# A macaron encoder layer: the mixing stage between its two feed-forward blocks written out in a new order

## What is computed

```python
x = x + 0.5 * swiglu(rmsnorm(x, ffn1_norm), ...)
h = rmsnorm(x, mix_norm)
p = h @ w_in                       # 1024 -> 3072: q | k | v | hyena x0 | x1 | v, 512 each
# differential attention, 4 heads, each with two 64-wide softmaxes over a T5 bias
attn = softmax(logits[0]) - lam * softmax(logits[1])
out = rmsnorm(attn @ v, subln_g) * (1.0 - lambda_init)      # norm over the 128 values of a head
# hyena: short convolution of width 3 on x0, x1, v; then
v = v * x1
v = irfft(rfft(v) * rfft(kernel)) + v * filt_bias           # kernel from a small MLP
y = rmsnorm_by_group(v * x0, out_g)                         # groups of 64 channels
x = x + concat([out, y]) @ w_out                            # 1024 -> 1024
x = x + 0.5 * swiglu(rmsnorm(x, ffn2_norm), ...)
x = rmsnorm(x, final_norm)
```

## Time and profile before

| | us |
|---|---|
| median of 3 runs (1060.88 to 1065.59) | 1061.97 |
| the profiled execution, its own time | 1061.0 |
| its span, first to last instruction | 1059.2 |
| TensorE busy | 1034.5 (98%) |
| VectorE busy | 569.8 (54%) |
| ScalarE busy | 335.2 (32%) |
| GpSimd busy | 60.7 (6%) |

### The profile page before, as it was taken

The page is one execution under the profiler, slowest core; times in us unless marked ns, Lnnn a source line. Parts: engine busy times, 40 slices in busy tenths (PEclk is TensorE's granted clock), DMA queues, the critical chain, the costliest instruction groups (busy, mean ns, idle before and its releaser), DMA issues. The chain is left out here.

```text
span 1059.2 us, 12002 instructions
## 1 busy us (share of the span) xinstructions
PE 1034.5 (98%) x4551; PEld 821.8 (78%) x4551; DVE 569.8 (54%) x722; ACT 335.2 (32%) x477; POOL 60.7 (6%) x57
## 2 busy tenths in 40 slices
PE   9999999999999999999999969999999999999996
PEld 8887888888777867777775558878888888888885
DVE  5545444454544458695876695764544444433332
ACT  6222222222222333444444203532222222222222
POOL 0000000000000010000000160300000000000000
PEclk9999999999999999999999989999999999999999
DMA  7743332333233361322211000323333333333322
GB/s 221 165 118 90 100 99 86 98 95 101 83 94 105 90 199 40 97 78 80 80 60 40 1 20 21 99 87 98 94 99 99 99 99 90 96 97 91 94 70 79
DMA packets 184460, 96.69 MB, mean 91 GB/s; under 512 B 14811, under 2 KB 181859, under 8 KB 184424
## 3 DMA queue, kind: packets, MB, share of 16 engines
q1 hardware_dynamic: 183160, 92.70, 30.2%
q0 software_dynamic: 352, 1.85, 0.6%
q10 hardware_dynamic: 912, 1.64, 0.5%
HBM read 94.07 MB, written 2.11 MB: 91 GB/s over the span
## 5 line engine op out<-in xcount | busy, mean ns | idle before, releaser
L1137 PE MATMUL bank<-x_hi,w_hi 128*128 128x512 f32 x880 | 347.0, 394 | 0.8 <-DVE x_lo L748 0.4
L1139 PE MATMUL bank<-x_hi,w_lo 128*128 128x512 f32 x880 | 342.6, 389 | 0.0
L1138 PE MATMUL bank<-x_lo,w_hi 128*128 128x512 f32 x880 | 342.6, 389 | 0.0
L713 DVE TENSOR_TENSOR w_lo<-raw,w_hi 128x1024 fp32r<-128x1024 f32 x168 | 203.6, 1212 | 220.9 <-ACT w_hi L447 216.5
L447 ACT CAST w_hi<-raw 128x1024 fp32r<-128x1024 f32 x168 | 172.3, 1026 | 167.4 <-PE bank L1139 131.8
L1137 PEld LDWEIGHTS bank<-x_hi,w_hi 128*128 128x128 f32 x880 | 165.2, 188 | 43.2 <-issue 7.0
L1139 PEld LDWEIGHTS bank<-x_hi,w_lo 128*128 128x128 f32 x880 | 165.2, 188 | 34.7
L1138 PEld LDWEIGHTS bank<-x_lo,w_hi 128*128 128x128 f32 x880 | 165.3, 188 | 34.6 <-issue 1.2
L1137 PE MATMUL bank<-h_hi,w_hi 128*128 128x512 f32 x352 | 137.3, 390 | 0.0
L1139 PE MATMUL bank<-h_hi,w_lo 128*128 128x512 f32 x352 | 137.0, 389 | 0.0
L1138 PE MATMUL bank<-h_lo,w_hi 128*128 128x512 f32 x352 | 136.9, 389 | 0.0
(11 more groups left out here) (207 smaller groups left out, 783.3 us busy)
## 6 DMA issues: line engine op xcount, KB each, us to landing
raw<-in_ffn_w_gate SPq DMA_DIRECT2D x44, 512.0 KB, 3.8
raw<-in_ffn_w_up SPq DMA_DIRECT2D x44, 512.0 KB, 3.7
raw<-in_ffn_w_down SPq DMA_DIRECT2D x32, 512.0 KB, 3.5
raw<-in_w_in SPq DMA_DIRECT2D x24, 512.0 KB, 3.7
raw<-in_ffn_w_down SPq DMA_DIRECT2D x16, 384.0 KB, 3.0
raw<-in_w_out SPq DMA_DIRECT2D x8, 512.0 KB, 3.4
x_nat<-in_x SPq DMA_DIRECT2D x4, 512.0 KB, 7.1
out<-o_nat SPq DMA_DIRECT2D x8, 256.0 KB, 2.9
```

The costliest lines, as they stand in the source:

```text
L713: nc.vector.tensor_tensor(w_lo[:, half, 0:kb, :], raw[:, slot, 0:kb, :], w_hi[:, half, 0:kb, :].bitcast(F32), ALU.subtract).then_inc(w_spl ...
L1137: nc.tensor.matmul(dst, w_hi[:, half, k, :], hi, start=first and k == 0, stop=False)
L1138: nc.tensor.matmul(dst, w_hi[:, half, k, :], lo, start=False, stop=False)
L1139: ins = nc.tensor.matmul(dst, w_lo[:, half, k, :], hi, start=False, stop=last and k == kb - 1)
```

## The change

- The tiles of the projection go in the order of a list `SEQ` of (kind, group) pairs: first x1 and v of the hyena for all four groups, then v, q, k of head 0, x0 of two groups, and so on head by head.
- The filters, the kernel spectra and the turning of the values (`turn_values`) stand between the first eight tiles. The forward transforms, the spectral products and the four inverse transforms stand between the heads of the attention. Products and both sums are all VectorE's; GpSimd's part is gone. The products are cut into small functions (`cross_products` and those behind it) that stand between `logits` and `combine` calls.
- The inverse transform goes by channel group: `inverse(g)` needs both frequency halves of the spectrum (`spec_set` at 2). `attend(2)` uses PSUM bank 4 behind `inverse(0)`, so it waits for `long_read`, which the first `long_out` sets.
- `logits` does the scaling, the bias and the row minimum in one instruction (`tensor_tensor_reduce`). `combine` has one pass over the row fewer, since the common factor of the first softmax is left to the norm.
- `attend` multiplies with `attn_t` as the stationary operand, in 128 columns, so a head's output has its queries on partitions. The sum of squares of the norm then comes out of ScalarE's accumulator (`attended`), the scale is a broadcast along the row (`att_scale`), and `turn_att` turns the result back. The column sums and spreads of the attention are gone; those of the hyena stay.
- The spectra need room, so SyncE writes `resid` (2 MB) to DRAM early in the stage and reads it back behind the last inverse transform; both transfers stand in the queue of the weight loads.
- The output tiles begin with the hyena half, and `OUT_TILES` and `OUT_BANKS` change: two pairs of residual blocks, the third and the fourth, are now handled behind one another at the last tile.

```diff
-OUT_TILES = [(0, 0), (0, 1), (0, 2), (1, 0), (1, 1), (1, 2), (0, 3), (1, 3)]
-OUT_DONE = [OUT_TILES.index((1, pair)) for pair in range(4)]
+OUT_TILES = [(1, 0), (1, 1), (0, 0), (1, 2), (0, 1), (1, 3), (0, 2), (0, 3)]
+OUT_DONE = [OUT_TILES.index((0, pair)) for pair in range(4)]
+SEQ = [(4, 0), (5, 0), (4, 1), (5, 1), (4, 2), (5, 2), (4, 3), (5, 3), (2, 0),
+       (0, 0), (1, 0), (3, 0), (3, 3), (2, 1),
...
@@ SyncE
+            for n, (m, g) in enumerate(SEQ):
+                load(w[:, :, m * D_ATT + g * P:m * D_ATT + (g + 1) * P], KD, N_MIX + n)
+                if n == 3:
+                    sp.wait_ge(resid_set, KD)
+                    sp.dma_start(resid_dram, resid[:]).then_inc(resid_saved, 16)
...
@@ VectorE
-                    nc.vector.scalar_tensor_tensor(logit[:, c, :], bank[2 + c][:], -(DK ** -0.5), near,
-                                                   ALU.mult, ALU.subtract).then_inc(logit_set, 1)
...
-                    nc.vector.tensor_reduce(soft[:, c:c + 1], logit[:, c, :], AX.X, ALU.min).then_inc(max_set, 1)
+                    nc.vector.tensor_tensor_reduce(logit[:, c, :], bank[2 + c][:], near, -(DK ** -0.5), LEAST,
+                                                   ALU.add, ALU.min, stat[:, c:c + 1]).then_inc(logit_set, 1)
...
-                link(nc.vector.tensor_scalar(prob[:, 1, :], prob[:, 1, :], soft[:, 6:7], None, ALU.mult))
+                link(nc.vector.scalar_tensor_tensor(stat[:, 3:4], s0, lam[:, 5:6], stat[:, 2:3], ALU.mult, ALU.mult))
...
+            project(20)
+            split(8, N_MIX + 22)
+            combine(2, 0)
+            taps(20)
+            logits(2, 1)
+            own_products(1)
+            combine(2, 1)
+            project(21)
+            split(8, N_MIX + 23)
+            imaginary(1)
+            logits(2, 2)
+            real(1)
+            combine(2, 2)
+            real_parities(1)
+            logits(2, 3)
+
+            project(22)
+            split(8, N_OUT)
+            imaginary_parities(1)
+            combine(2, 3)
+            split_qk(3, 0)
+            project(23)
+            split(8, N_OUT + 1)
+            split_qk(3, 1)
+            long_out(0)
...
@@ TensorE
+            def attend(h):
                 pe.wait_ge(attn_set, NT * (h + 1))
+                if h < 2:
+                    pe.wait_ge(spec_read, h + 1)
+                else:
+                    pe.wait_ge(long_read, (1, 3)[h - 2])
...
-                    ins = nc.tensor.matmul(bank[6][:], v_nat[:, kt, :], attn_t[:, kt, :], start=kt == 0, stop=kt == NT - 1)
+                    for qb in range(NT):
+                        ins = nc.tensor.matmul(bank[6][:, qb * P:(qb + 1) * P], attn_t[:, kt, qb * P:(qb + 1) * P], v_nat[:, kt, :],
+                                               start=(kt, qb) == (0, 0), stop=(kt, qb) == (NT - 1, NT - 1))
...
+            def inverse(g):
+
+                pe.wait_ge(spec_set, 2)
...
+            project(20)
+            scores(2, 1)
+            project(21)
+            scores(2, 2)
+            project(22)
+            scores(2, 3)
+
+            inverse(0)
+            project(23)
+            attend(2)
+            turn_v(3)
+            pe.wait_ge(qk_split, 8)
+            scores(3, 0)
+            inverse(1)
```

More of the change, by code:

```diff
@@ new lines, in _ @@
+            project(8)
+            split(8, N_MIX + 10)
+            project(9)
+            split(8, N_MIX + 11)
+            project(10)
+            split(8, N_MIX + 12)
+            split_qk(0, 0)
+            split_qk(0, 1)
+            cosines(0)
+            sines(0)
+            logits(0, 0)
+            project(11)
+            split(8, N_MIX + 13)
+            combine(0, 0)
+            taps(11)
+            logits(0, 1)
+            cross_products(0)
+            combine(0, 1)
+            project(12)
@@ new lines, in _ @@
+            split(8, N_MIX + 14)
+            taps(12)
+            logits(0, 2)
+            own_products(0)
+            project(13)
+            split(8, N_MIX + 15)
+            combine(0, 2)
+            imaginary(0)
+            logits(0, 3)
+            project(14)
+            split(8, N_MIX + 16)
+            combine(0, 3)
+            project(15)
+            split(8, N_MIX + 17)
+            split_qk(1, 0)
+            split_qk(1, 1)
+            real(0)
+            real_parities(0)
@@ new lines, in _ @@
+            combine(3, 3)
+            long_out(3)
+            hy_inverse(0)
+            att_scale(0)
+            for g in range(3):
+                hy_scale(g)
+            hy_inverse(1)
+            hy_low(0)
+            hy_low(1)
+            hy_scale(3)
+            hy_low(2)
+            hy_low(3)
+            att_scale(1)
+            att_low(0)
+            att_low(1)
+            split(8, N_OUT + 2)
+            att_low(2)
+            att_low(3)
+            for n in range(2, KD):
@@ new lines, in _ @@
+            project(7)
+            project(8)
+            for g in range(NG):
+                turn_values(g)
+            project(9)
+            project(10)
+            turn_v(0)
+            forward(0)
+            pe.wait_ge(qk_split, 2)
+            scores(0, 0)
+            project(11)
+            scores(0, 1)
+            project(12)
+            scores(0, 2)
+            project(13)
+            scores(0, 3)
+            project(14)
+            project(15)
+            attend(0)
+            turn_v(1)
@@ new lines, in _ @@
+            scores(2, 3)
[5 more added lines that the diff above has]
+            scores(3, 0)
+            inverse(1)
+            scores(3, 1)
+            inverse(2)
+            scores(3, 2)
+            col_sums(0)
+            col_sums(1)
+            scores(3, 3)
+            inverse(3)
+            col_sums(2)
+            attend(3)
+            col_sums(3)
+            for g in range(3):
+                spread(g)
@@ L1478, in _ @@
+            out_tile(0, between=lambda: spread(3))
+            turn_att(0)
+            turn_att(1)
+            out_tile(1)
+            turn_att(2)
+            turn_att(3)
+            for n in range(2, KD):
+                out_tile(n)
+            pe.wait_ge(resid_set, KD + 4)
             gate_up(1, N_FF2, 0, first=True)
```

988 lines of the change are left out of this document (513 added, 475 removed), and 3 rows, old and new, of the table SEQ.

## The result

The changed kernel takes 1077.06 us (median of four runs, 1073.92 to 1077.21) against 1061.61 us for the kernel before. The ratio is 1.0131 with an interval of 1.0099 to 1.0162: 1.3% slower. A second set of four runs gave 1074.98 us, ratio 1.0129 (1.0109 to 1.0149). Forecast were 1070.5 us and a range of 1055 to 1080, with 1064 to 1077 for the likeliest case; the first median lies at the upper end of that, the second inside it.

The account below looks back on a forecast made before the run. TensorE, busy 98% of the span, bounds the kernel through its work, waits and clock. 20.2 us won against 30.4 of new waits and clock is 10.2 more, taken as 9.5: 1061.0 becomes 1070.5 us, range 1055 to 1080.

Parts of the forecast that it names:

- 1, the waits as counted: Whole kernel: the new waits stand as counted, 1070.5 us, alone 1064 to 1077; chance 0.50.
- Rival 4: `logits`: `tensor_tensor_reduce` takes 1.2 us with 512 columns, 8 us more in all, 1078 us; chance 0.07.
- rival 5: Early projections: the 2 MB `resid` write delays the fifth tile by the bound, 6 us more, 1077 us; chance 0.05.
- what the forecast had taken off its sum: Whole kernel: 10.2 us more was taken as 9.5, since chains for head 3 and the end partly overlap.
- Work: TensorE: 8.3 us of attention sums and spreads gone, 2.2 of transposes and 1.5 for `v` products new; 4.6 us less.
- The waits that go: Mixing stage: 9.3 us for the spectral sums and 1.1 ahead of the first scores vanish, 10.4 us.
- The new waits: TensorE, first tiles to tail: waits counted from VectorE's and ScalarE's pieces, 26.4 us, the largest 8.1 at `inverse(0)`.
- The clock: TensorE: three dips go, 5.2 us; new ones of 2.35 behind the inverse transform's wait and 1.7 at the end.
- `logits`: VectorE: the joined instruction takes 0.65 us with the read of its result, a pair 1.3; bounds 0.6 and 1.2.
- The DMAs: `resid` write and read back: no cost taken; the other bound is the fifth projection tile 8 us late.
- rival 2: `inverse(0)` wait under about 4 us, no clock fall there, `scores(0, 3)` wait gone: 1061 us; chance 0.22.
- rival 3: Bank guard and end chain cost little, VectorE being early there: 1055 us and less; chance 0.16.

Follow-up runs that it names:

- experiment 8: Changed kernel with the last output tiles reordered, (0, 2) ahead of (1, 3): 1073.93 us, ratio 1.0119.
- Experiment 3: Changed kernel with 29 idle matmuls ahead of `inverse(0)` and 15 ahead of `attend(2)`, filling TensorE's waits: 1072.07 us, ratio 1.0097.
- experiment 5: Kernel before with only the joined `logits` instruction added, the bias scaled once ahead of the stage: 1057.36 us, ratio 0.9964.
- experiment 10: Changed kernel with `project(23)` before `inverse(0)`, first inverse transform in its own bank, `taps(12)`, `taps(20)` later, stage end and last output tiles reordered: 1051.29 us, ratio 0.9898.
- experiment 1: Changed kernel with `project(23)` moved ahead of `inverse(0)` on TensorE, nothing else: 1062.38 us, ratio 1.0008.

## Why the prediction was right, and where its sum was wrong

The direction, the rival that stands (1, the waits as counted) and the range held. The time was 6.6 us over the forecast, 4.5 in the second set of runs. Rivals 4 and 5 had said 1078 and 1077, so the time alone doesn't choose; the traces do. The profiled execution's span grew by 15.6 us where 9.5 were forecast. Of the 6.1 us between, +6.5 is the clock in the stage, +2.7 the start of the kernel, which the forecast left out, -2.2 the waits, -1.6 the work, and +0.7 what the forecast had taken off its sum. Step by step:

**Work.** Forecast 4.6 us less, measured 6.2 as the part left over; with the spread of that number over profiles, 1 to 7, the forecast stands. The row of the products with `v` has 18.2 us for 128 instructions now, dips included, against the 16.4 of the earlier trace rows; +1.5 was right within what the dips let one see. The 16 new transposes take 2.1, forecast 2.2.

**The waits that go.** Forecast 10.4. This was right for the two it named, but the stage before held 14.2 us of idle time in all, and some of the rest was rearranged too.

**The new waits.** Forecast and measured, in order: the first eight tiles 1.0 and 2.2 (0.86 at the second tile, 0.71 at the third, 0.66 at `kernel_sums(0)`); `scores(0, 3)` 2.6 and 2.6; the inverse transform 8.1 and 7.0; `attend(2)` 3.7 and 3.8; `attend(0)` and `attend(1)` together 1.4 and 2.1 (1.32 + 1.41, less the 0.7 that they had before); `scores(3, 3)` 1.8 and 1.3; `attend(3)` 0.4 and 0.3; `col_sums(3)` 1.3 and 0.9; the first output tile 3.0 and 3.0, its third slice 1.4 and 1.4; the tail 1.7 and 1.8 (2.2 for `x_lo`, less the 0.4 of before). Counting pieces from VectorE's rows put eight of these eleven within half a us. The waits of L1306 for `w_lo` belong to the first tiles, not to the tail, against what experiment 8 had expected. The idle time of the stage grew by 13.8, where the forecast's 26.4 - 10.4 is 16.0. The inverse transform's wait is 1.1 short of its count although VectorE took just the 22.1 us: TensorE took 15.1 us for its own pieces, not 14.0, since it waits 0.57 us for the third pair of `logits` ahead of `scores(2, 3)` (the third wait of L1423), and some tenths lie between its pieces.

**The clock: the term that was mis-sized.** The prediction let 5.2 us of dips go and put 2.35 + 1.7 = 4.05 in their place, a gain of 1.15. Measured in the stage: 5.8 before and 11.1 after in the profiled execution, a loss of 5.3; in the second profile 9.2, a loss of 3.4; over all executions 12.3 and 16.8, a loss of 4.5, or of 3.7 against the 13.1 of the other 19. I gave a dip to the wait of 8 us and to the end, because before had shown them there, and none to the waits of 2.6, 3.8 and 1.3 us. Each of these had one behind it or around its end: 1.7, 2.8 and 3.4 us lost. Experiment 3 shows for the two at `inverse(0)` and `attend(2)` that standing still is the cause. For `scores(0, 3)` it is only likely. For the stretch behind `scores(3, 3)` it is open: the waits of up to 1.4 us at `attend(0)` and `attend(1)` have no dip behind them in any of ten profiles, this one has one in all ten. In the changed kernel 16 matmuls of two columns stand right ahead of it (622.4 to 624.3 us), which the others lack; nothing was run on that.

**`logits`.** Forecast 0.65 each, bounds 0.6 and 1.2; measured 0.62 from one to the next, with the read of the result hidden in it. Rival 4, at 1.2, is out. With one source in PSUM, as here, it costs hardly more than a plain sum (0.62 against 0.60). The Trainium skill ("Vector Engine (DVE) Microarchitecture Reference", Points that are easy to get wrong) gives half the throughput for the scalar-tensor-tensor shape of instruction with two sources in SBUF that are not bf16. That the joined instruction has this shape is my reading, and no run has it at 512 columns with both sources in SBUF. What I undervalued is what it is worth: experiment 5 gives 4.5 us for it on the kernel before.

**The DMAs.** TensorE shows no wait for `raw` or `resid` in the stage, as I had taken. The issues (line's tensors, queue, size, us to landing):

```profile
resid_dram<-resid SPq DMA_DIRECT2D x1, 2048.0 KB, 8.2
resid<-resid_dram SPq DMA_DIRECT2D x1, 2048.0 KB, 8.6
```

2 MB landed in 8.2 us, well under the bound of 14.8 (four times 3.7) from the earlier trace rows. But the load of the fifth tile, issued at 380.34 right behind the write, took 17.7 us, near the bound of 18.5 for both; it landed at 398.0, and ScalarE rounded it at 398.61. In the second profile ScalarE's rounding did wait for this landing. So rival 5 is out, since TensorE lost nothing by it, but the margin was 0.6 us. ScalarE's own queue, ahead of the second tile's rounding:

```profile
380.41 1.83 ACTq L534 DMA_DIRECT2D decay_b<-in_c_decay  x1
...
382.27 1.62 ACTq L535 DMA_DIRECT2D w<-in_hy_f_w  x1
383.99 1.05 ACT L433 CAST w_hi<-raw 128x1024 fp32r<-128x1024 f32 x1 [2.79 <-issue]
```

In the kernel before the same two issues take 0.52 and 0.53 us and this rounding comes after 0.39 us of waiting. The 0.86 us that TensorE waits at the second tile is for the `w_lo` made from this rounding. That the write, issued 0.4 us ahead of them, slows these issues is likely; no run leaves it out of this order.

**Rivals 2 and 3.** The prediction said that it would be wrong if the inverse transform's wait were under 4 us, and that rival 3 needed VectorE early at the bank guard. Neither came. Their times can be reached, but by another way than theirs, with VectorE no faster: the same work, with one projection moved by one place, is at 1062.4, with rival 2's 1061 within its runs, and experiment 10 goes below rival 3's 1055.

What I did not see, though the rows for it were there: I wrote that `project(23)` "stands behind it and cannot fill the gap", and took this as given. 5.66 us of ready work behind a wait of 8 us is not only a line in the sum, it is the repair.

## What to carry to other kernels

When a change moves waits about, write down for each wait of the bound engine which ready work stands right behind it in program order: a 7 us wait with 5.7 us of independent work behind it was most of this change's loss, and exchanging two lines gave back 13 to 15 us. Put a cost in TensorE's clock behind every wait of the size of 2.6 us and more, not only the longest: here 1.5 to 3.4 us each where it came. A shorter wait can have one, too (3.4 behind one of 1.3), and others like it had none. In experiment 10, which kept only waits of up to 1.4 us, 5.1 us was lost in place of 11.1. Split a change that has an order and some edits in it: here two edits were gains of 4.2 and 4.5 us, hidden under a rest that cost some 21 us as it was written and was worth about 3 us once repaired.

## What was not expected of the hardware

**A short wait can be followed by a dip that begins when the wait is over.** TensorE in the changed kernel around 500 us (start, duration, line, operation, tiles):

```profile
498.08 0.49 PE L1423 MATMUL bank<-k_hi,q_hi 64*128 64x512 f32 x1 [2.58 <-DVE stat L970]
...
499.58 0.50 PE L1306 MATMUL bank<-x_hi,w_hi 128*128 128x512 f32 x1
499.92 0.54 PE L1307 MATMUL bank<-x_lo,w_hi 128*128 128x512 f32 x1
500.25 0.63 PE L1308 MATMUL bank<-x_hi,w_lo 128*128 128x512 f32 x1
...
503.24 0.48 PE L1306 MATMUL bank<-x_hi,w_hi 128*128 128x512 f32 x1
```

The wait of 2.58 us ends at 498.08. The matmuls behind it run at full speed until about 500, then 0.43 us apart instead of 0.23 until 503.2. Whoever looks for the cause of a dip at the instructions inside it finds a plain projection.

**The loss often comes in like portions.** Of the 53 dips between 370 and 710 us in the fourteen profiles, 26 lost 1.7 us and 8 lost about twice that, 3.3 to 3.4; the others lie between 1.5 and 3.2. Examples: 1.71 at 569 to 574 and at 648 to 652 in the kernel before, 1.7 at 500 in the changed one, 3.4 at 626 to 634, 3.4 at 607 to 615 in experiment 10.

**And the same code has them or not.** Behind one wait of 2.6 us the dip was there in six profiles of eight. The clock goes with the spread of the executions: the fastest of experiment 1's ten has 1060.5 us at a mean clock of 0.994, the slowest 1064.8 at 0.989, and 0.005 of the span is 5.3 us. This is likely a good part of why executions of one kernel spread over 3 us, and why a repair of 2 us could not be told from nothing with four executions, while the small repairs together took 11 us off experiment 1.
